# A hybrid decoder step on one core: last eleven convolution steps and the bonus product moved into the scan, the channel norm one inversion level later

## What is computed

```python
h = rms_norm(x, norm_mix); p = h @ w_in
y_a, wkv_new, row_new = rwkv7_mix(p[..., :SHIFT_COLS], ...)   # 8 heads of 64: a scan over tokens
y_b, buf_new = conv_mix(p[..., SHIFT_COLS:], ...)             # 512 channels
x = x + concat(y_a, y_b) @ w_out
x = x + moe_ffn(rms_norm(x, norm_ffn), ...)                   # top 4 of 32 experts

def conv_mix(...):
    u = u[..., :C_B] * sigmoid(u[..., C_B:])
    z = causal depthwise convolution of width 31 over u, + dw_bias
    z = layer_norm(z, conv_ln_w, conv_ln_b)                   # over the 512 channels of a token
    return z * sigmoid(z), ...
```

## Time and profile before

| what | value |
|---|---|
| median of 3 runs | 1258.36 us (1258.32 to 1260.72) |
| the profiled execution | 1259.54 us |
| its span in the trace | 1257.6 us |
| TensorE matmul busy | 1205.8 us (96%) |
| VectorE, ScalarE, POOL busy | 449.1, 190.6, 61.5 us |
| bytes moved | 428.90 MB, mean 341 GB/s |
| w_out: four loads of 1 MB | 8.1 us from issue to landing (median) |

### The profile page before, as it was taken

The page is one execution under the profiler, slowest core; times in us unless marked ns, Lnnn a source line. Parts: engine busy times, 40 slices in busy tenths (PEclk is TensorE's granted clock), DMA queues, the critical chain, the costliest instruction groups (busy, mean ns, idle before and its releaser), DMA issues.

```text
span 1257.6 us, 19283 instructions
## 1 busy us (share of the span) xinstructions
PE 1205.8 (96%) x8077; PEld 550.8 (44%) x8077; DVE 449.1 (36%) x982; ACT 190.6 (15%) x375; POOL 61.5 (5%) x103
## 2 busy tenths in 40 slices
PE   7999799999899999999999999999999999999995
PEld 5667589866333333333333333333333333333332
DVE  5657754241263222323332222322332322222224
ACT  2362224122210010100010100100001000100012
POOL 0303441010000000000000000000000000000000
PEclk8999899999799999999999999999999999999999
DMA  9321210178699999999999999999999999999994
GB/s 260 123 68 46 66 79 4 32 238 299 279 429 422 425 428 425 429 427 429 429 427 429 429 428 428 428 429 429 427 429 428 429 429 427 430 428 429 426 427 168
DMA packets 54478, 428.90 MB, mean 341 GB/s; under 512 B 13231, under 2 KB 26975, under 8 KB 29838
## 3 DMA queue, kind: packets, MB, share of 16 engines
q1 hardware_dynamic: 52986, 427.92, 82.4%
q10 hardware_dynamic: 1436, 0.16, 0.1%
HBM read 424.93 MB, written 3.11 MB: 340 GB/s over the span
## 4 chain that ended last, share of the span: by engine, by line
PE 59%; DMA 19%; DVE 1%; ACT 0%; issue 0%; ACTq 0%; DVEq 0%
PE bank L1722 40%; DMA ring<-in_w_up_dram 19%; PE bank L1702 6%; PE bank L1776 5%; PE bank L1709 2%; PE bank L1660 1%; PE bank L1607 1%; PE bank L1730 1%; PE bank L1748 1%; PE bank L1665 0%; PE bank L1597 0%; DVE arena L2072 0%; DVE arena L2066 0%; PE bank L1622 0%; DVE arena L2012 0%
## 5 line engine op out<-in xcount | busy, mean ns | idle before, releaser
L1722 PE MATMUL bank<-ring,arena 128*64 128x512 f32 x1536 | 344.5, 597 | 8.2 <-DMA ring<-in_w_up_dram 6.5
L1722 PE MATMUL bank<-arena 128*64 128x512 f32 x1536 | 342.5, 593 | 6.4 <-DMA arena<-in_w_up_dram 6.4
L1722 PEld LDWEIGHTS bank<-ring,arena 128*64 128x64 f32 x1536 | 109.7, 137 | 220.6 <-issue 202.8
L1722 PEld LDWEIGHTS bank<-arena 128*64 128x64 f32 x1536 | 108.7, 136 | 217.5 <-issue 199.7
L1998 DVE TENSOR_SCALAR arena<-bank 128x512 f32<-128x512 f32 x32 | 22.1, 691 | 382.9 <-PE bank L1730 382.9
L2012 DVE TENSOR_TENSOR arena<-arena,bank 128x512 f32<-128x512 f32 x186 | 113.5, 679 | 1.6 <-PE bank L1776 1.6
L512 PE MATMUL bank<-arena,ring 128*128 128x336 f32 x352 | 104.8, 456 | 1.1 <-DVE arena L646 1.1
L1702 PE MATMUL bank<-arena 128*64 128x512 f32 (+1 forms) x384 | 92.1, 615 | 1.1 <-DVE arena L1919 1.1
L1776 PE MATMUL bank<-arena 64*128 64x512 f32 (+1 forms) x384 | 91.1, 606 | 0.7 <-issue 0.7
L2002 DVE TENSOR_SCALAR arena<-bank 128x512 f32<-128x512 f32 x32 | 22.1, 691 | 176.3 <-PE bank L1730 176.3
L512 PEld LDWEIGHTS bank<-arena,ring 128*128 128x128 f32 x352 | 67.8, 194 | 35.2 <-issue 2.8
(11 more groups left out here) (350 smaller groups left out, 816.7 us busy)
## 6 DMA issues: line engine op xcount, KB each, us to landing
ring<-in_w_gate_dram SPq DMA_DIRECT2D x32, 2048.0 KB, 25.2
arena<-in_w_up_dram SPq DMA_DIRECT2D x32, 2048.0 KB, 28.2
arena<-in_w_down_dram SPq DMA_DIRECT2D x32, 2048.0 KB, 31.5
ring<-in_w_down_dram SPq DMA_DIRECT2D x32, 2048.0 KB, 31.7
arena<-in_w_gate_dram SPq DMA_DIRECT2D x32, 2048.0 KB, 26.9
ring<-in_w_up_dram SPq DMA_DIRECT2D x32, 2048.0 KB, 29.4
ring<-in_w_in_dram SPq DMA_DIRECT2D x11, 1024.0 KB, 5.2
ring<-in_w_out_dram SPq DMA_DIRECT2D x4, 1024.0 KB, 8.1
```

Of the source, the lines that this page charges most:

```text
L1722: mm = M.matmul(bank[64 * hb:64 * hb + 64, b, :], tokens(cc), w[:, c, 512 * hb:512 * hb + 512], start=(cc == 0), stop=(w3 == 2 and cc == K ...
```

## The change

The constant CONV_LATE = 11 is new. The mixer does 113 of the 124 convolution steps, and the last eleven are done by VectorE in the scan: two behind the masks of pair 0, two behind those of pair 1 (with the bonus product behind these), and seven behind those of pair 2. The mean product goes from the head of the scan to the end of level 1, the variance product from behind pair 1 to the end of level 2; the centring and the squares go behind level 1, the variance and its root behind level 2, reciprocal, product and affine part behind level 3, the sigmoid behind level 4 and the last multiply behind level 5. SP's loads of w_out and POOL's Kx wait for the eleven steps.

```diff
@@ mixer, VectorE
-                for _ in conv:
-                    pass
+                convolve(4 * CW - CONV_LATE - 113)
@@ scan, SP
+                sp.wait_ge(S["conv_step"], CONV_LATE)
                 for t in range(UNITS_IN, UPRE):
                     load_unit(sp, t)
@@ scan, POOL
                 pool.wait_ge(S["seq4_ready"], 1)
+                pool.wait_ge(S["conv_step"], CONV_LATE)
@@ scan, ScalarE
-                for j in range(4):
-                    act.wait_ge(S["z_centered"], j + 1)
-                    nc.scalar.activation(zsq[:, j, :], zT[:, j, :], ACT.Square).then_inc(S["z_squared"], 1)
...
                     if l == 1:
+                        for j in range(4):
+                            act.wait_ge(S["z_centered"], j + 1)
+                            nc.scalar.activation(zsq[:, j, :], zT[:, j, :], ACT.Square).then_inc(S["z_squared"], 1)
+                    if l == 2:
                         act.wait_ge(S["zvar_ready"], 1)
                         nc.scalar.activation(zvar, zvar, ACT.Sqrt).then_inc(S["zroot_ready"], 1)
-                    if l == 3:
-                        act.wait_ge(S["z_affine"], 1)
-                        nc.scalar.activation(zsq, zT, ACT.Sigmoid).then_inc(S["z_sig"], 1)
...
                         level(l, p)
+                    if l == 4:
+                        act.wait_ge(S["z_affine"], 1)
+                        nc.scalar.activation(zsq, zT, ACT.Sigmoid).then_inc(S["z_sig"], 1)
@@ scan, TensorE
-                for j in range(4):
-                    mm = M.matmul(bank[:, 7, 0:NT], ones, zT[:, j, :], start=(j == 0), stop=(j == 3))
-                mm.then_inc(S["zmean_done"], 1)
...
-                    if p == 1:
-                        pe.wait_ge(S["z_squared"], 4)
-                        for j in range(4):
-                            mm = M.matmul(bank[:, 7, 0:NT], ones, zsq[:, j, :], start=(j == 0), stop=(j == 3))
-                        mm.then_inc(S["zvar_done"], 1)
...
                     for p in range(NP3):
+                        if (l, p) == (2, 2):
+                            pe.wait_ge(S["z_centered"], 4)
                         level_a(l, p)
+                    if l == 1:
+                        pe.wait_ge(S["conv_step"], CONV_LATE)
+                        pe.wait_ge(S["at_ready"], number_t[(1, 2)] + 1)
+                        for j in range(4):
+                            mm = M.matmul(bank[:, 7, 0:NT], ones, zT[:, j, :], start=(j == 0), stop=(j == 3))
+                        mm.then_inc(S["zmean_done"], 1)
+                    if l == 2:
+                        pe.wait_ge(S["z_squared"], 4)
+                        pe.wait_ge(S["at_ready"], number_t[(2, 2)] + 1)
+                        for j in range(4):
+                            mm = M.matmul(bank[:, 7, 0:NT], ones, zsq[:, j, :], start=(j == 0), stop=(j == 3))
+                        mm.then_inc(S["zvar_done"], 1)
@@ scan, VectorE
-                V.tensor_tensor(bonT, bonT, vT, ALU.mult)
+                def conv_late():
+                    for k, (h, tap, r) in enumerate([(h, tap, r) for h in range(2) for tap in range(CW)
+                                                     for r in range(2)][4 * CW - CONV_LATE:]):
...
+                        if k >= 2:
+                            dve.wait_ge(S["conv_step"], k - 1)
+                        V.scalar_tensor_tensor(dst, ext[:, j, :, tap:tap + SL], w, dst, ALU.mult, ALU.add)\
+                            .then_inc(S["conv_step"], 1)
+                        yield
...
-                dve.wait_ge(S["zmean_done"], 1)
-                for j in range(4):
-                    V.scalar_tensor_tensor(zT[:, j, :], bank[:, 7, 0:NT], -1.0 / CB, zT[:, j, :],
-                                           ALU.mult, ALU.add).then_inc(S["z_centered"], 1)
...
-                dve.wait_ge(S["zvar_done"], 1)
-                V.tensor_scalar(zvar, bank[:, 7, 0:NT], 1.0 / CB, LN_EPS, ALU.mult, ALU.add).then_inc(S["zvar_ready"], 1)
+                    for _ in range((2, 2, 7)[p]):
+                        next(conv)
+                    if p == 1:
+                        V.tensor_tensor(bonT, bonT, vT, ALU.mult)
...
                     if l == 1:
+                        dve.wait_ge(S["zmean_done"], 1)
...
+                    if l == 2:
+                        dve.wait_ge(S["zvar_done"], 1)
...
+                    if l == 3:
                         dve.wait_ge(S["zroot_ready"], 1)
                         V.reciprocal(zvar, zvar).then_inc(S["zinv_ready"], 1)
-                    if l == 2:
...
```

More of the change, by code:

```diff
@@ L44 @@
 UNIT = 2048
+CONV_LATE = 11
 RING = 8
@@ L822, in rkq @@
             return RKq[64 * i:64 * i + 64, :, j * NT + ts:j * NT + ts + n]
-        names = ["v_turned", "vtok_ready", "hat_ready",
+        names = ["conv_step", "v_turned", "vtok_ready", "hat_ready",
                  "zmean_done", "z_centered", "z_squared", "zvar_done", "zvar_ready", "zroot_ready", "zinv_ready",
@@ L1030, in level_a @@
                         pe.wait_ge(S["n_read"], 3)
-                        pe.wait_ge(S["zvar_ready"], 1)
                     else:
@@ L1045, in _ @@
                     for p in range(NP3):
+                        if (l, p) == (2, 2):
+                            pe.wait_ge(S["z_centered"], 4)
                         level_a(l, p)
+                    if l == 1:
[10 more added lines that the diff above has]
+                        mm.then_inc(S["zvar_done"], 1)
                 level_g(4, 0)
                 level_g(4, 1)
-                pe.wait_ge(S["at_ready"], number_t[(2, 2)] + 1)
+                pe.wait_ge(S["zvar_ready"], 1)
                 for j in range(NPAIR):
@@ L1171, in _ @@
                 V.tensor_tensor(seq4, seqrow[:, 0:4], seqrow[:, 4:8], ALU.add).then_inc(S["seq4_ready"], 1)
-                V.tensor_tensor(bonT, bonT, vT, ALU.mult)
+                def conv_late():
+                    for k, (h, tap, r) in enumerate([(h, tap, r) for h in range(2) for tap in range(CW)
+                                                     for r in range(2)][4 * CW - CONV_LATE:]):
+                        j = 2 * h + r
+                        w = vecW[:, 4 * tap + j:4 * tap + j + 1]
+                        dst = by_eight(zT[:, j, :])
+                        if k >= 2:
[3 more added lines that the diff above has]
+                        yield
+                conv = conv_late()
                 for p in range(NP3):
@@ L1216, in _ @@
                     if l == 1:
+                        dve.wait_ge(S["zmean_done"], 1)
+                        for j in range(4):
+                            V.scalar_tensor_tensor(zT[:, j, :], bank[:, 7, 0:NT], -1.0 / CB, zT[:, j, :],
+                                                   ALU.mult, ALU.add).then_inc(S["z_centered"], 1)
+                    if l == 2:
+                        dve.wait_ge(S["zvar_done"], 1)
+                        V.tensor_scalar(zvar, bank[:, 7, 0:NT], 1.0 / CB, LN_EPS, ALU.mult, ALU.add)\
+                            .then_inc(S["zvar_ready"], 1)
+                    if l == 3:
                         dve.wait_ge(S["zroot_ready"], 1)
                         V.reciprocal(zvar, zvar).then_inc(S["zinv_ready"], 1)
-                    if l == 2:
                         dve.wait_ge(S["zinv_ready"], 1)
@@ L1228, in _ @@
                 level(4, 1)
-                dve.wait_ge(S["z_sig"], 1)
-                V.tensor_tensor(zT, zT, zsq, ALU.mult).then_inc(S["zT_ready"], 1)
                 level(5, 0)
@@ L1234, in _ @@
                 V.tensor_copy(Wc5, bank1(4)).then_inc(S["wc5_ready"], 1)
+                dve.wait_ge(S["z_sig"], 1)
+                V.tensor_tensor(zT, zT, zsq, ALU.mult).then_inc(S["zT_ready"], 1)
                 dve.wait_ge(S["zT_ready"], 1)
```

## The result

**1264.45 us** median of seven runs (1263.47 to 1267.55), against 1258.32 of seven runs of the kernel before (1254.42 to 1260.72): ratio 1.0052, 95% interval 1.0038 to 1.0067, slower by 6.1 us. Forecast were 1263.2 and "slower". The profiled execution took 1263.47 us, its span is 1261.6. Size and sign came out. Of the terms behind them several did not, and one of the prediction's own signs of being wrong was met: level 1 started over 7 us sooner. What the right total hides is the larger part of this document.

A forecast was written before the change was run, and what follows sets the result against it. The first expert's start on TensorE, plus a constant, was taken to set the end. Known terms summed to +2.0 us; clock 1.7, port 0.5 and code 0.6 made +4.8, on the median of 1258.36: 1263.2, range 1259.0 to 1267.5.

The forecast's parts named there:

- Barrier, -0.45: Mixer's end: SP's stores hold the barrier, so it comes 0.9 us sooner, worth 0.45 at half clock.
- rival E: Mixer's end: SP's stores don't hold the barrier and all 5.35 us of the run come off, 1258.8; chance 0.08.
- Opening, -2.4: Scan's head: removing the 4.82 us mean product gains 2.4; the low clock's price of 2.4 falls on the first turns.
- rival B: First 5 us of the scan: small turns aren't slowed by the low clock, 1260.3, no measurable change; chance 0.14.
- Variance product, -2.46: Loop over the three tile pairs: the variance product leaves TensorE there, gaining 2.46 us.
- I cost both at nothing; that cover gone, they would cost 0.3: Pair loop: two steps after each of the first two pairs, bonus product behind the second, hidden under TensorE's turns.
- Seven steps ahead of the masking, +2.6: After the third pair: seven steps delay level 1's first masking, so its third product loses 2.6; TensorE stands 3 us.
- the port, +0.5: Third pair: POOL's two additions wait for VectorE's run of seven steps, costing 0.5 us, bounds 0 and 2.2.
- rival D: VectorE's steps wait for POOL instead of the other way round: 1.7 us more, 1264.9; chance 0.05.
- Clock, +1.7: After TensorE's 3 us stand in level 1: one stretch at half speed, 1.7 us lost, bounds nothing or 3.4.
- Rival A: TensorE's stand in level 1: the clock stays up through it, 3.1 us more than before, 1261.5; chance 0.20.
- TensorE's code, +0.6: Beside the squarings: code reads queue behind the late w_out load; one stall goes, two can come, bounds -1.2 and +2.5.

The follow-up runs named there:

- number 8: The kernel before with VectorE's last eleven convolution steps left out altogether: 1258.6 us, one run, against 1257.07 for the kernel before.
- Numbers 1: The changed kernel with all 124 convolution steps back in the mixer and the bonus product back at the scan's head, only the norm moved: 1255.55 us, 0.9983.
- 6: The kernel before with one wait added, so that SP issues the four w_out loads only at the inversion's last product: 1261.26 us, 1.0034.
- number 7: The changed kernel with all eleven steps behind level 1's maskings and the bonus product behind level 2's: 1259.77 us, 1.0023.
- number 3: The changed kernel with POOL's three instructions for the third pair held until the eleven steps are done: 1264.06 us, one run.
- number 5: The changed kernel with ten unused filler products in TensorE's stand before the third product of level 1: 1267.01 us, 1.0071.
- 4: The changed kernel with twenty unused filler products between the second and third product of level 1; they outlasted the stand: 1272.03 us, 1.0104.
- 9: The changed kernel with all eleven steps behind level 1, the bonus product behind level 2, and SP's eleven stores moved to the scan's head: 1254.07 us, 0.9968.
- 10: Kernel 9 with the convolution input's four blocks in reverse order, so three w_out loads go at the scan's start, one after the steps: 1251.82 us, 0.9954.
- 11: Kernel 9 with w_out's four loads spaced out, the first when the steps are done and the others at later waits: 1251.04 us, 0.9951.

## Why the prediction came out, step by step

The total was off by 1.3 us, with errors on both sides.

- **Barrier, -0.45: right that SP holds it** (number 8), so rival E falls. The start is 1.2 sooner in this pair of profiles, 0.7 by TensorE's shorter idle at the barrier (5.68 against 6.39) and the rest by a mixer that ended sooner. Numbers 1 and 6 put the steps' part of it at 0.2, so the 0.9 read from one profile of before was at the upper end.
- **Opening, -2.4: right in kind, 1.4 too small.** The 4.82 of the mean product go, and the 160 turns take 6.83 in place of 5.12 at the low clock, so they are slowed by 1.7, and rival B falls. Start and opening together bring 4.25 (156.62 against 160.87), where I had 2.85: "if the clock rises at the same time as before" was wrong. It rose at 153.9, where before had 0.50 until 156.0, and the start is 1.2 sooner in this pair of profiles, not 0.9. The 1.4 is half of what rival B had, without B's reason.
- **Variance product, -2.46: right.** The pair loop is 3.9 shorter; 1.23 of that is the code stall that moved away, 0.2 no term of mine. With start and opening it brings level 1 8.2 us sooner. The prediction had some 5, and had named over 7 as a sign that B or E is true: neither is, so the sign was badly set. Its terms by themselves, 2.85 and 2.46 and the stall of 1.23, already gave 6.5.
- **"I cost both at nothing; that cover gone, they would cost 0.3": wrong.** The four steps and the bonus in the pair loop took 6.8 us instead of 3.5. VectorE ended the third pair 2.58 behind the start of level 1's first product (175.92 against 173.34), in number 7 0.90 (173.21 against 172.31): 1.7 late. Number 7 has none of it in the loop, and has no lag. The count had taken their durations (0.97 for two steps, 1.55) from the earlier trace rows, where POOL was idle.
- **Seven steps ahead of the masking, +2.6, and the port, +0.5: the step that failed is the port.** The stand is 6.95, and level 1's third product loses 6.6. 2.6 of it are the term as it was; 1.7 is the lag above; 2.3 is the contention inside the seven steps (5.74 against 3.43, number 3), which I had POOL pay, by one row in which POOL had waited. It was rival D's mechanism, to which I gave 0.05. The Trainium skill, page "SBUF — State Buffer", section "Who interferes with whom", had said that either side can be the one shut out, whichever starts first; the runs agree that VectorE can be the loser. POOL's first operation of each pair ran its plain 1.09, and the other two 1.36 and 1.42 in place of the 1.09 and 1.27 of number 7, beside steps of 0.56 to 1.57. So both sides pay, VectorE more; the records look as if the two took turns. A row on one loser should have given an even chance to the other one.
- **End of level 1, +1.65: right**, +1.8 in number 1 and number 7. After shows +4.3, the rest being the low clock.
- **End of level 2, +3.1: right**, +2.9 in after and in number 1.
- **Clock, +1.7: too small.** In the profile 10.2 us at 0.50 with 5.68 of work, 2.8 lost, and 3.4 us more of work at 218.7, 1.7 lost. Number 5 shows that the first of them goes when TensorE has no stand. Rival A falls: in none of the seven runs is the mean granted clock over 0.984. What brings the later one isn't settled: no idle of note stands before it, and the profiles of numbers 3 and 4 have one at the same product.
- **TensorE's code, +0.6: right mechanism, in this profile not paid.** That a read queues behind the load was the guess from one idle, and numbers 6, 7, 9, 10 and 11 and the packets of the instruction queue bear it out. By itself, the load's move costs 3.3 us (number 6), where I had 0.6; the slow stretch whose cause is open is in these 3.3. Against the Trainium skill, page "Runtime: NRT & Kernel Launch", section "Instruction fetch mechanics", whose rule has such reads mostly hidden, stand stalls of 0.61 to 2.58 beside the late load of 4 MB; there the measurement decides. Where no load runs beside them, the scan's profiles have 0.3 us at most put down to "issue", so there the trace agrees. In the profile of after no such stall shows. The load (181.6 to some 191) fell into the slow stretch, and number 5, where that stretch was gone, has the stall; so in that profile the cost of the clock covers that of the code, and adding them was wrong.
- **What was costed as hidden was hidden**: reciprocal, product and affine part end by 214.71, the next masking by 215.91, and TensorE needs it at 218.35, behind the state product; the last column is no longer than before.

At the state product the profile has 5.4 us lost, at the final stage 7.3 (261.9 against 254.65, the slow stretch at 218.7 in it). The medians differ by 6.1: the router's clock gave 3.3 us back in this pair of profiles, whose times differ by 3.9. Against my sum of 4.8, the lag adds 1.7, the contention 1.8 and the first slow stretch 1.1; start and opening take off 1.4, the code stall that didn't come 1.8, the rest of the pair loop and levels 1 to 3 0.9: 5.3 at the state product, and 1.7 more for the second slow stretch. That the forecast came within 0.1% is luck in good part: at the state product 4.6 us that I had missed met 4.1 that I had too much.

## What to carry to other kernels

Work moved under another engine must be priced with its new neighbour: a fused step of 0.49 us on VectorE took up to 1.57 beside POOL, and a product of 1.55 took 2.62. Whatever a moved step reads holds its buffer longer, and so moves a load; ask what that load will then run beside. And before taking work off an engine at a barrier, find who comes last: here eleven stores of SP, whose move is worth 5.7 us once VectorE is done early, and VectorE's early end 0.2 to 0.8 without it.

## What the runs showed of the hardware

- VectorE and POOL slow each other: 5.74 us for seven steps beside three POOL operations, 3.43 without, and POOL's 1.36 and 1.42 in place of 1.09 and 1.27. Both sides pay.
- A read of TensorE's code behind a load of 4 MB cost 0.4 to 2.6 us in ten profiles (0.42 in number 8, 2.58 in number 5) and nothing visible in after's; the idle is put down to "issue" alone, and ends 1.2 to 1.5 us behind the end of a packet of the instruction queue. Single loads of 1 MB cost 0 to 0.8, three together 0.55. With the clock at 0.50 behind it, a stall of 1.64 cost 4.7 in all (number 7), one of 2.58 4.2 (number 5).
- An idle of 2.13 us at the same place left the clock at 1.00 in two profiles (before and number 8) and at 0.50 in one with w_out's load beside it (number 6). Through idles of 1.8 us at the opening it stayed up in all three kernels that had them; after idles of 5.6 and more it was at 0.50 in each.
- The kernel before ran between 1252.5 and 1261.6 us over the 61 runs beside the experiments, and the profiles of one stage's unchanged code differ in where the clock falls. A difference of 2 us between two profiles, taken by itself, shows nothing. The mean granted clock of a run goes with its time (correlation -0.69 to -0.85 in the three groups of runs of before), so it is worth reading for every run and not only for the profiled one.
